# Retention's rotary q and k in a hybrid decoder trunk: the two halves of a head in tiles of their own, in place of a rotation product on TensorE

## The reference, cut to what matters

```python
def apply_rope(x, cos, sin):
    half = x.shape[-1] // 2
    x1, x2 = x[..., :half], x[..., half:]
    return jnp.concatenate([x1 * cos - x2 * sin, x1 * sin + x2 * cos], axis=-1)

def retention_branch(q, k, v, g, cos, sin):
    q = apply_rope(q.reshape(bsz, s, 8, 64), cos, sin)      # and k in the same way
    scores = einsum('bnchd,bnshd->bnhcs', qc, kc) * inner_decay
    y_inner = einsum('bnhcs,bnshe->bnche', scores, vc)
    ...                                                     # the state between chunks, group norm, silu(g) * y
```

## Time and profile before

| | |
|---|---|
| time, median of 3 runs | 983.22 us (983.09 to 984.32) |
| the profiled execution | 986.28 us, of which 984.5 are the span |
| PE busy | 955.5 us, 97% |
| DVE busy | 718.4 us, 73% |
| ACT busy | 525.1 us, 53% |
| mean granted TensorE clock | 0.982 of full |
| moved by DMA | 206.39 MB, mean 210 GB/s |

### The profile page before, as it was taken

The page is one execution under the profiler, slowest core; times in us unless marked ns, Lnnn a source line. Parts: engine busy times, 40 slices in busy tenths (PEclk is TensorE's granted clock), DMA queues, the critical chain, the costliest instruction groups (busy, mean ns, idle before and its releaser), DMA issues.

```text
span 984.5 us, 17698 instructions
## 1 busy us (share of the span) xinstructions
PE 955.5 (97%) x6976; PEld 888.6 (90%) x6976; DVE 718.4 (73%) x958; ACT 525.1 (53%) x701; POOL 43.6 (4%) x85
## 2 busy tenths in 40 slices
PE   7999999999998999999989999999999999999997
PEld 7889989999987999999969999899999799999996
DVE  4689766676677898786975966676657789676765
ACT  4346855455446655544673485643445656554554
POOL 0000000000000100000000000000000000000000
PEclk7799999999999999999999999999999999999999
DMA  9985755566572786776637864556736557555451
GB/s 352 378 256 184 248 170 165 193 193 215 174 267 87 276 306 238 255 254 231 238 111 213 274 198 167 154 187 211 242 110 236 192 200 270 193 186 178 151 187 44
DMA packets 134141, 206.39 MB, mean 210 GB/s; under 512 B 6336, under 2 KB 104384, under 8 KB 133952
## 3 DMA queue, kind: packets, MB, share of 16 engines
q1 hardware_dynamic: 122416, 162.07, 50.0%
q0 software_dynamic: 11520, 41.95, 11.7%
q10 hardware_dynamic: 144, 1.51, 0.4%
HBM read 204.46 MB, written 1.05 MB: 209 GB/s over the span
## 4 chain that ended last, share of the span: by engine, by line
PE 89%; ACT 3%; DVE 3%; DMA 2%; SPq 1%; issue 1%; DVEq 0%; ACTq 0%
PE banks L1682 79%; DMA raw<-in_w_in 2%; PE banks L1698 1%; DVE w_lo L1091 1%; PE banks L1968 1%; PE banks L1971 1%; SPq L473 1%; PE banks L1706 1%; PE banks L1812 1%; PE banks L1794 1%; DMA raw<-in_ada_rows 1%; ACT w_hi L583 1%; PE banks L1742 1%; ACT h L632 1%; PE banks L1831 1%
## 5 line engine op out<-in xcount | busy, mean ns | idle before, releaser
L1682 PE MATMUL banks<-h_lo,w_hi 128*128 128x256 f32 x1504 | 427.3, 284 | 8.9 <-DVE w_lo L1091 6.0
L1682 PE MATMUL banks<-h_hi,w_lo 128*128 128x256 f32 x1504 | 421.4, 280 | 0.0
L1682 PE MATMUL banks<-h_hi,w_hi 128*128 128x256 f32 x1504 | 421.1, 280 | 0.0
L1682 PEld LDWEIGHTS banks<-h_lo,w_hi 128*128 128x128 f32 x1504 | 284.3, 189 | 13.6 <-DVE w_lo L1091 7.3
L1682 PEld LDWEIGHTS banks<-h_hi,w_lo 128*128 128x128 f32 x1504 | 284.3, 189 | 2.3 <-issue 1.4
L1682 PEld LDWEIGHTS banks<-h_hi,w_hi 128*128 128x128 f32 x1504 | 284.1, 189 | 0.0
L1091 DVE TENSOR_TENSOR w_lo<-raw,w_hi 128x2048 fp32r<-128x2048 f32 x96 | 219.4, 2289 | 68.0 <-ACT w_hi L583 67.7
L583 ACT ACTIVATE w_hi<-raw 128x2048 fp32r<-128x2048 f32 x96 | 182.6, 1912 | 116.3 <-PE banks L1682 95.9
L1597 DVE TENSOR_TENSOR w_lo<-raw,w_hi 128x2048 fp32r<-128x2048 f32 x42 | 96.0, 2285 | 18.3 <-ACT w_hi L960 18.3
L1573 DVE SCALAR_TENSOR_TENSOR EF<-banks,par,EF 128x254 f32<-128x254 f32 (+1 forms) x176 | 76.8, 478 | 43.4 <-ACT EF L941 38.8
L960 ACT ACTIVATE w_hi<-raw 128x2048 fp32r<-128x2048 f32 x42 | 80.4, 1914 | 33.9 <-PE banks L1682 33.9
(11 more groups left out here) (282 smaller groups left out, 1262.0 us busy)
## 6 DMA issues: line engine op xcount, KB each, us to landing
raw<-in_w_in SPq DMA_DIRECT2D x52, 1024.0 KB, 6.0
raw<-in_ffn_w_up SPq DMA_DIRECT2D x44, 1024.0 KB, 5.1
adw<-in_ada_rows POOLq DMA_DIRECT2D x80, 512.0 KB, 4.8
raw<-in_ffn_w_down SPq DMA_DIRECT2D x22, 1024.0 KB, 5.0
raw<-in_w_out SPq DMA_DIRECT2D x8, 1024.0 KB, 6.8
raw<-in_ret_wo SPq DMA_DIRECT2D x4, 1024.0 KB, 5.0
raw<-in_lru_wo SPq DMA_DIRECT2D x4, 1024.0 KB, 6.5
raw<-in_mla_wo SPq DMA_DIRECT2D x4, 1024.0 KB, 6.9
```

The lines of the kernel that those rows point to most:

```text
L1682: ins = MM(ps, lhs, rhs, start=first and n == 0, stop=last and n == 2)
```

## The change

The columns of q and k in `w_in` are put in another order outside of the kernel, into an array `rotary` of 1024 x 1024 per layer: for each group of four heads first the first halves of the four, then the second halves. A tile of 128 partitions then holds one half of four heads, and a bank holds both halves of four heads. So the partner of each element is on the same partition in the other tile: `rope_sum` takes it from `tmp` by two operations of 256 columns, a subtraction and an addition, and PE makes no rotation. A head's 64 features lie in 32 partitions of two tiles, so each score product becomes two of 32 rows, added up in the bank; `ret_scores(h)` issues those of heads h and h + 1 in turn. The sums stand directly behind their parts on DVE. Blocks q and k are read from `rotary`.

```diff
+def rotary_columns(w_in):
+    qk = w[:, :, 1024:2048].reshape(n_l, d, 4, HEADS // 2, 2, 32).transpose(0, 1, 2, 4, 3, 5)
...
-        block(("q", i), lambda l, i=i: win(l, o_rq + BW * i, BW), DK, BW)
+        block(("q", i), lambda l, i=i: rows("rotary", l, 0, DK, BW * i, BW), DK, BW)
...
-                act.wait_ge(rot_ps.s, rot_ps.at(l, 4))
+                act.wait_ge(rope.s, rope.at(l, 4))
...
                 def rope_sum(i):
-                    dve.wait_ge(rot_ps.s, rot_ps.at(l, i + 1))
                     dve.wait_ge(rot_c.s, rot_c.at(l, i + 1))
-                    V.tensor_tensor(AB[:, 2 * i:2 * i + 2, :], AB[:, 2 * i:2 * i + 2, :], rope_bank(i), ALU.add).then_inc(rope.s, 1)
+                    dve.wait_ge(rot_t.s, rot_t.at(l, i + 1))
+                    first, second = (tmp[:, 2 * (i % 2) + b, :] for b in range(2))
+                    V.tensor_tensor(AB[:, 2 * i, :], AB[:, 2 * i, :], second, ALU.subtract)
+                    V.tensor_tensor(AB[:, 2 * i + 1, :], AB[:, 2 * i + 1, :], first, ALU.add).then_inc(rope.s, 1)
...
-                rotate(0)
-                rotate(1)
+                pe.wait_ge(tables_in, 16)
+                pe.wait_ge(v_ev.s, v_ev.at(l, 2))
                 two_tiles(l, J[("lx", 0)], 3)
-                rotate(2)
                 two_tiles(l, J[("lx", 1)], 1)
-                rotate(3)
...
-                def ret_score(h):
-                    r = slice(64 * (h % 2), 64 * (h % 2) + 64)
-                    q, k = AB[r, h // 2, :], AB[r, 4 + h // 2, :]
-                    bank = (5, 0)[h % 2]
+                def ret_scores(h):
                     if h >= 2:
-                        pe.wait_ge(rs_p.s, rs_p.at(l, h - 1))
-                    MM(PS[:, bank, 0:T], k[:, 0:P], q, start=True, stop=True)
-                    MM(PS[:, bank, T:T + P], k[:, P:T], q[:, P:T], start=True, stop=True).then_inc(rs_ps.s, 1)
+                        pe.wait_ge(rs_p.s, rs_p.at(l, h))
+                    for keys, queries, cols in ((slice(0, P), slice(0, T), slice(0, T)), (slice(P, T), slice(P, T), slice(T, T + P))):
+                        for part in range(2):
+                            for n in (h, h + 1):
+                                r, t = slice(32 * (n % 4), 32 * (n % 4) + 32), 2 * (n // 4) + part
+                                ins = MM(PS[:, (5, 0)[n % 2], cols], AB[r, 4 + t, keys], AB[r, t, queries], start=part == 0,
+                                         stop=part == 1)
```

More of the change, by code:

```diff
@@ L109, in vectors @@
     return packed
+def rotary_columns(w_in):
+    w = np.asarray(w_in)
+    n_l, d, _ = w.shape
+    qk = w[:, :, 1024:2048].reshape(n_l, d, 4, HEADS // 2, 2, 32).transpose(0, 1, 2, 4, 3, 5)
+    return np.ascontiguousarray(qk.reshape(n_l, d, 1024))
 def first_rows(ada_w):
@@ L158, in trunk_kernel @@
     for i in range(2):
-        block(("q", i), lambda l, i=i: win(l, o_rq + BW * i, BW), DK, BW)
+        block(("q", i), lambda l, i=i: rows("rotary", l, 0, DK, BW * i, BW), DK, BW)
     for i in range(2):
-        block(("k", i), lambda l, i=i: win(l, o_rk + BW * i, BW), DK, BW)
+        block(("k", i), lambda l, i=i: rows("rotary", l, 0, DK, W + BW * i, BW), DK, BW)
     for i in range(2):
@@ L318, in trunk_kernel @@
         g_th, g_ev = sig("g_th", 2), sig("g_ev", 2)
-        rot_ps, rot_t, rot_c, rope = sig("rot_ps", 4), sig("rot_t", 4), sig("rot_c", 4), sig("rope", 4)
+        rot_t, rot_c, rope = sig("rot_t", 4), sig("rot_c", 4), sig("rope", 4)
         rs_ps, rs_p, rs_av = sig("rs_ps", 8), sig("rs_p", 8), sig("rs_av", 8)
@@ L1282, in rope_parts @@
                     if i >= 2:
-                        dve.wait_ge(rot_ps.s, rot_ps.at(l, i - 1))
+                        dve.wait_ge(rope.s, rope.at(l, i - 1))
                     two = tmp[:, 2 * (i % 2):2 * (i % 2) + 2, :]
@@ L1300, in _ @@
                 rope_parts(0)
+                rope_sum(0)
                 mixer_split(l, 5)
                 rope_parts(1)
+                rope_sum(1)
                 mixer_split(l, 6)
@@ L1305, in _ @@
                 rope_parts(2)
-                rope_sum(0)
+                rope_sum(2)
                 rope_parts(3)
-                rope_sum(1)
+                rope_sum(3)
                 if l == 0:
@@ L1350, in _ @@
                 lru_taps(0)
-                rope_sum(2)
                 mixer_split(l, 9)
@@ L1354, in _ @@
                     softplus(1)
-                rope_sum(3)
                 lru_taps(1)
@@ L1822, in _ @@
                 lru_gate(3)
-                def ret_score(h):
-                    r = slice(64 * (h % 2), 64 * (h % 2) + 64)
-                    q, k = AB[r, h // 2, :], AB[r, 4 + h // 2, :]
-                    bank = (5, 0)[h % 2]
+                def ret_scores(h):
                     if h >= 2:
-                        pe.wait_ge(rs_p.s, rs_p.at(l, h - 1))
-                    MM(PS[:, bank, 0:T], k[:, 0:P], q, start=True, stop=True)
-                    MM(PS[:, bank, T:T + P], k[:, P:T], q[:, P:T], start=True, stop=True).then_inc(rs_ps.s, 1)
+                        pe.wait_ge(rs_p.s, rs_p.at(l, h))
[5 more added lines that the diff above has]
+                                         stop=part == 1)
+                                if part == 1 and cols.start == T:
+                                    ins.then_inc(rs_ps.s, 1)
                 def ret_av(h):
@@ L1848, in _ @@
                 pe.wait_ge(lr_ev.s, lr_ev.at(l, 1))
-                ret_score(0)
-                ret_score(1)
+                ret_scores(0)
                 pe.wait_ge(c_sq.s, c_sq.at(l, 3))
@@ L1869, in _ @@
                 ret_av(1)
-                ret_score(2)
-                ret_score(3)
+                ret_scores(2)
                 pe.wait_ge(g_ev.s, g_ev.at(l, 1))
@@ L1875, in _ @@
                 ret_av(3)
-                ret_score(4)
-                ret_score(5)
+                ret_scores(4)
                 pe.wait_ge(cn.s, cn.at(l, 1))
@@ L1881, in _ @@
                 ret_av(5)
-                ret_score(6)
-                ret_score(7)
+                ret_scores(6)
                 def uq(i):
@@ L2199 @@
     for name, a in (("ada_rows", np.ascontiguousarray(np.swapaxes(inputs["ada_w"], 1, 2))), ("vectors", vectors(inputs)),
-                    ("ada_first", first_rows(inputs["ada_w"])), ("c_cols", np.ascontiguousarray(inputs["c"].reshape(-1, P).T))):
+                    ("ada_first", first_rows(inputs["ada_w"])), ("rotary", rotary_columns(inputs["w_in"])), ("c_cols", np.ascontiguousarray(inputs["c"].reshape(-1, P).T))):
         arrays[f"in_{name}"] = a
```

## The result

| | before | changed |
|---|---|---|
| median | 983.16 us (981.42 to 986.36, 8 runs) | 988.71 us (984.34 to 992.19, 8 runs) |
| ratio | | 1.0052, interval 1.0032 to 1.0073 |
| profiled execution | 986.28 | 988.71 |
| mean granted clock | 0.982 | 0.976 |

The change makes the kernel slower by 0.5%. The forecast was 983.4 (981.6 to 986.2) and no change: wrong, by 5.3 us and outside its range.

The account below looks back on a forecast made before the run. PE, busy 97%, was taken to bound the kernel. Layer 0 +1.2 (scores 2.6, gain 1.4), layer 1 -0.84 (2.6 - 3.44), DMA -0.2: +0.2 us on the median 983.22, so 983.4, range 981.6 to 986.2.

Parts of the forecast that it names:

- The rotations left PE: Rotation products L1794, 0.86 us each, four per layer, leave PE: 3.44 us per layer, 6.9 in all.
- A pair costs 1.51: Scores of two heads: 1.51 us instead of 0.86, heads overlapping, one head's parts not; 5.2 us more in all.
- A sum costs 0.87 (0.79 forecast): DVE's rotary sum as two operations of 256: 0.79 us, 0.19 more than 0.60.
- DVE holds c0 in layer 0: PE, through lx1 at 81.91, would wait for DVE's split of block c0 and start it at 83.62.
- from k0 to the scores 1.26 us are gained of 3.44 (1.4 forecast): Layer 0 would keep only 1.4 us of the 3.44 saved on rotations, because DVE is late with c0.
- No new wait came in layer 1, at c2, the gates or L1866: Layer 1 keeps all 3.44 us and c2's lead still covers; a wait at gates or L1866 would refute the forecast.
- I take 0.2 off q1: Layer 0's q1 transfer, read from 4 KB instead of 27 KB rows, lands 0.2 us sooner; bounds 0 and 0.4.
- Rival 1: PE's clock falls in two more places, in longer thin score stretches with idle rows: +3.3 us, 986.5; chance 0.14.
- Rival 2: The two heads of a score pair don't overlap, 2.81 us per pair: 994 us; chance 0.05.
- rival 3: All four strips' score products overlap, so the 5.2 us cost vanishes: 978.2 us; chance 0.05.
- rival 4: DVE not late in layer 0 (981.4), and clock not lost in layer 1 (both 979.8); chance 0.08.

Follow-up runs that it names:

- changed again: The changed kernel measured a second time, unaltered, for a second profile; ratio to the kernel before 1.0042.
- scores twice: The cost half alone: kernel before, rotation products kept, each score two products; 32 rows each 1.0072 (992.72 us), 64 rows each 1.0048 (990.17 us).
- four heads: The changed kernel with scores of four heads at once, each in its own 32-row strip and bank; ratio to before 0.9961, 980.21 us.
- scores away: The changed kernel with the first pair of scores one block earlier on PE, away from the column sums; ratio to before 1.0021, 986.74 us.
- the four with fillers: Unread dense PE products added per layer behind the last scores: seven, before 1.0072, changed 1.0118; four, before 1.0060, changed 1.0058.
- no rotations: The kernel before without its four rotation products per layer, scores still 64 rows; ratio 0.9946, 980.45 us.
- the two with thin stretches: The kernel before with 112 thin PE stretches and dense products behind its output, column sums 4.4 us, then 2.3; changed-style pairs fell 14, then 10 of 14.
- c0's split first: The changed kernel with c0's low half made on DVE ahead of the second angles and softplus in layer 0; ratio to before 1.0052.

## Why the prediction was wrong, point by point

**Right.** The rotations left PE. A pair costs 1.51, and only different strips overlap. A sum costs 0.87 (0.79 forecast). DVE holds c0 in layer 0 (83.72 in the second profile, 83.62 forecast); from k0 to the scores 1.26 us are gained of 3.44 (1.4 forecast). No new wait came in layer 1, at c2, the gates or L1866. The structure by itself is as good as unchanged. Take the falls out of three profiles, and give back 2.1 where q1 came early: before 986.28 - 3 x 1.55 = 981.6; changed 988.71 - 6 x 1.55 + 2.1 = 981.5; changed again 987.79 - 4 x 1.55 = 981.6. With the work that a run adds or drops taken out too (5.2, 6.0, 3.5 and -6.0 us), the profiles of scores twice, four heads, scores away and the four with fillers leave 981.1 to 981.9; in that of before with four fillers a fall at 41.4 counts as well, since q1 was early there and PE at work. So added work, falls and q1 account for the profiled times to within half a microsecond. The forecast was +0.2, or +0.4 without the 0.2 of the table.

**The transfer.** "I take 0.2 off q1": the first profile gives 2.1, the second nothing. Landings by kernel don't show an effect of the table. The reason that the Trainium skill offered, in "DMA: Bandwidth & Descriptors", How a descriptor splits into AXI transactions, is thus not seen here; 0.2 is too small to be excluded.

**The step that failed: the clock was counted at nothing.** The sum has no term for it: it put work and waits on the time of before and left the falls as they were there. Rival 1 allowed for two more with 0.14. By an estimate from the times there are 4.6 / 1.55, about 3 more, in an execution. There was a sign of the spread in the prediction's own numbers: its profile, with three falls, was 3.1 us above the median, which is the price of two. The rival's place and reason were right for a part. The falls of all profiles, counted by place:

| place | kernels as before there | kernels as changed there |
|---|---|---|
| behind the first scores and sums, both layers (a double one is two) | 7 in 12 | 16 in 12 |
| the pauses of 2.0 us at 248 and 724 | 1 in 8 | 8 in 8 |
| the pause at c0 | none there | 3 in 7 |
| the pause at 512 | 2 in 4 | 0 in 4 |

(First row: before, its two fillers, no rotations and the two with thin stretches; changed, again, c0's split first, 32 rows twice and its two fillers. Second and fourth: before, no rotations and the two with thin stretches; changed, again, c0's split first and scores away. Third: changed, again, four heads, scores away, changed with either filler, no rotations.)

A sum from it: 2 x 0.75 x 1.55 = 2.3 for the scores, 2 x 0.875 x 1.55 = 2.7 for the later pauses, 0.43 x 1.55 = 0.7 for c0, -0.8 for 512, together 4.9; the two comparisons gave 1.0052 and 1.0042, 4.6 us. The table is of few executions, and the thin stretches by themselves give the scores 0.9 rather than 2.3, so the shares are rough.

The prediction held that the moment decides, but only for the stretch at the scores. What it missed is that an edit in one place decides the falls in others that it doesn't touch. In the kernel before, the later pauses mostly kept the clock; three pairs of scores, 2.0 us longer, between the column sums and these pauses put them where they lost it (also in both runs of the cost alone, 4 in 4), and 1.7 us of filler moved them there or back again. The last two runs show this in times, and in rows of one execution each. The table of distances bears it out; why some distances are good is not shown.

The Trainium skill has the basis of it in "TensorE: Matmul & The Clock Gate", What's actually happening: the chip judges PE's activity on a schedule that runs free of the kernel's start. The traces agree in so far as the same work at the same place meets both clocks: c0 fell in the first profile of the changed kernel and not in its second, and behind the first sums of layer 0 the kernel before kept its clock and, with thin stretches behind its output, twice lost it. That a free schedule is the reason no run here shows.

Rival 2 (no overlap of the two heads), rival 3 (all four overlap in the changed order) and rival 4 (DVE not late, clock kept in layer 1) are refuted: a pair takes 1.51 us, PE waits for c0 in both profiles (to 81.46 and 83.72), and the fall in layer 1 was double.

## What to carry to other kernels

A change that leaves PE's work the same can still cost half a percent through its clock: list each thin stretch and pause of PE of 2 us and more, and treat each as a fall with a chance, since one profile shows one draw. Keep products that use few rows away from column sums and waits, and put as many strips in flight as there are strips and free banks: four heads at 32 rows cost what two cost. Before one blames a change, add a little dense work to both kernels at the same place, in two or three sizes; if their gap moves with one of them, part of it was the moment. Here four products closed it and seven did not.

## What was not expected of the hardware

- Work that shifts a pause can pay for most of itself: 3.5 us of useless products cost the changed kernel about 1.1 and the kernel before 5.9.
- Pairs of scores with two heads' products on v in front, 1.7 to 2.3 us long, never lost the clock (28 stretches), a pause of 1.6 us never (14), one of 2.1 us 8 times in 14.
- Two parts of 64 rows with sums behind them lost less clock (6 of 14) than one part (9 of 13); the difference is within chance.
- One transfer of 1 MB issued at 31 us took 11.2 to 14.1 or 16.3 us to land, by execution, with the same kernel text ahead of it; PE gains or loses 2 us by it.
